# Rotating the scanned states on GpSimd in two halves per part, with four products of a half ahead of its difference and sum

## What is computed

```
u = h.astype(F32).reshape(n, l, N_SSM_GROUPS, SSM_GROUP)
bu_re = jnp.einsum('nlgc,gpc->nlgp', u, bb_re)
bu_im = jnp.einsum('nlgc,gpc->nlgp', u, bb_im)
...
_, _, xr, xi = lax.associative_scan(complex_affine_combine, (a_r, a_i, bu_re, bu_im), axis=1)
y = (jnp.einsum('nlgp,gcp->nlgc', xr, c_re.astype(F32))
     - jnp.einsum('nlgp,gcp->nlgc', xi, c_im.astype(F32)))
...
z = jax.nn.gelu(y).astype(h.dtype)
zz = z @ w_glu
```

## Time and profile before

| | |
|---|---|
| median of 3 runs | 1167.6 us (1167.45 to 1169.94) |
| the profiled execution's own time | 1169.49 us |
| its span, first to last instruction | 1167.7 us |
| busy over the span: PE | 1116.0 us (96%) |
| DVE | 725.3 us (62%) |
| ACT | 458.3 us (39%) |
| POOL | 397.2 us (34%) |
| mean granted TensorE clock | 0.990 |

### The profile page before, as it was taken

The page is one execution under the profiler, slowest core; times in us unless marked ns, Lnnn a source line. Parts: engine busy times, 40 slices in busy tenths (PEclk is TensorE's granted clock), DMA queues, the critical chain, the costliest instruction groups (busy, mean ns, idle before and its releaser), DMA issues. The chain is left out here.

```text
span 1167.7 us, 25260 instructions
## 1 busy us (share of the span) xinstructions
PE 1116.0 (96%) x9826; PEld 1092.5 (94%) x9826; DVE 725.3 (62%) x1132; ACT 458.3 (39%) x752; POOL 397.2 (34%) x624
## 2 busy tenths in 40 slices
PE   5999879999999999799998889999999999999998
PEld 5998669999999999799997779999999999999998
DVE  5874745688875258877436944457777433777632
ACT  5424773454442134344344333335444312444310
POOL 7013007999998879700337840000000000000000
PEclk9998999999999999899999999999999999999999
DMA  8322002333353332423756523222223322222322
GB/s 260 127 73 65 2 1 75 132 119 126 128 190 136 122 122 77 144 90 110 271 154 192 135 86 99 90 90 72 92 95 102 112 69 90 90 90 90 117 86 100
DMA packets 47959, 129.05 MB, mean 111 GB/s; under 512 B 12320, under 2 KB 17680, under 8 KB 47904
## 3 DMA queue, kind: packets, MB, share of 16 engines
q1 hardware_dynamic: 42272, 114.68, 30.1%
q0 software_dynamic: 5632, 13.63, 3.7%
HBM read 109.79 MB, written 18.21 MB: 110 GB/s over the span
## 5 line engine op out<-in xcount | busy, mean ns | idle before, releaser
L1547 PE MATMUL ps<-hx_hi,w_hi 128*128 128x260 f32 x1600 | 457.4, 286 | 22.5 <-DVE w_lo L1032 18.4
L1549 PE MATMUL ps<-hx_hi,w_lo 128*128 128x260 f32 x1600 | 454.4, 284 | 0.0
L1548 PE MATMUL ps<-hx_lo,w_hi 128*128 128x260 f32 x1600 | 453.2, 283 | 0.0
L722 ACT ACTIVATE w_hi<-w_raw 128x1024 fp32r<-128x1024 f32 (+1 forms) x156 | 175.6, 1126 | 445.7 <-PE ps L1549 441.4
L1547 PEld LDWEIGHTS ps<-hx_hi,w_hi 128*128 128x128 f32 x1600 | 303.7, 190 | 25.9 <-DVE w_lo L1032 11.9
L1549 PEld LDWEIGHTS ps<-hx_hi,w_lo 128*128 128x128 f32 x1600 | 303.6, 190 | 0.0
L1548 PEld LDWEIGHTS ps<-hx_lo,w_hi 128*128 128x128 f32 x1600 | 303.5, 190 | 0.1
L1032 DVE TENSOR_TENSOR w_lo<-w_raw,w_hi 128x1024 fp32r<-128x1024 f32 (+1 forms) x156 | 208.6, 1337 | 98.1 <-ACT w_hi L722 97.9
L1547 PE MATMUL ps<-hid_hi,w_hi 128*128 128x260 f32 x704 | 199.1, 283 | 0.5 <-DVE hid_lo L1372 0.5
L1548 PE MATMUL ps<-hid_lo,w_hi 128*128 128x260 f32 x704 | 198.7, 282 | 0.0
L1549 PE MATMUL ps<-hid_hi,w_lo 128*128 128x260 f32 x704 | 198.7, 282 | 0.0
(11 more groups left out here) (284 smaller groups left out, 1576.3 us busy)
## 6 DMA issues: line engine op xcount, KB each, us to landing
w_raw<-in_wup SPq DMA_DIRECT2D x88, 512.0 KB, 3.3
w_raw<-in_wdn SPq DMA_DIRECT2D x32, 704.0 KB, 4.1
w_raw<-in_wglu SPq DMA_DIRECT2D x16, 512.0 KB, 3.4
w_raw<-in_wqkv SPq DMA_DIRECT2D x12, 512.0 KB, 3.4
w_raw<-in_wo SPq DMA_DIRECT2D x8, 512.0 KB, 3.3
g_scr<-rec POOLq DMA_DIRECT2D x8, 512.0 KB, 3.1
c_scr<-rec POOLq DMA_DIRECT2D x8, 512.0 KB, 3.3
wst<-g_scr SPq DMA_DIRECT2D x8, 512.0 KB, 7.7
```

The source lines that it names most:

```text
L722: act.activation(w_hi[b][:, 0:kt * P], w_raw[b][:, 0:kt * P], ACT.Copy).then_inc(hi_done, 1)
L1547: pe.matmul(out, wh, xh, start=(k == 0), stop=False)
L1548: pe.matmul(out, wh, xl, start=False, stop=False)
L1549: ins = pe.matmul(out, wl, xh, start=False, stop=(k == kt - 1))
```

## The change

The six instructions of a part's rotation on POOL, each over 256 columns, become twelve over 128 columns. The part is cut into two halves of two pairs of groups (`h` 0 and 1). In a half all four products are issued, into four separate pieces of `ptmp`; then POOL waits for them once; then come the difference and the sum. The first half ends in a wait of POOL for its own sum, since the second half writes the same pieces of `ptmp`; the second half's sum gives `x_done`. The copy that follows, the loop over the parts and every other engine's list stay as they are. `ptmp` has 512 columns before and after.

```
-                t0 = ptmp[:, 0:JQ * 64].rearrange("p (q c) -> p q c", q=JQ)
-                t1 = ptmp[:, JQ * 64:JQ * 128].rearrange("p (q c) -> p q c", q=JQ)
-                out = x4[:, JQ * j:JQ * (j + 1), :, NS + 1:NS + 1 + NC]
                 pool.wait_ge(sem("z_done"), j + 1)
                 tt = pool.tensor_tensor
-                tt(t0, z[:, 0], e[0], ALU.mult)
-                after(tt(t1, z[:, 1], e[1], ALU.mult))
-                after(tt(out[:, :, 0, :], t0, t1, ALU.subtract))
-                tt(t0, z[:, 1], e[0], ALU.mult)
-                after(tt(t1, z[:, 0], e[1], ALU.mult))
-                tt(out[:, :, 1, :], t0, t1, ALU.add).then_inc(sem("x_done"), 1)
+                for h in range(2):
+                    g = slice(2 * h, 2 * h + 2)
+                    z = zst[j % 2][:].rearrange("p (r q c) -> p r q c", r=2, q=JQ)[:, :, g]
+                    e = [t[:].rearrange("p (q c) -> p q c", q=JQ)[:, g] for t in rots[j % ROTS]]
+                    t0, t1, t2, t3 = [ptmp[:, n * 128:n * 128 + 128].rearrange("p (q c) -> p q c", q=2)
+                                      for n in range(4)]
+                    out = x4[:, JQ * j + 2 * h:JQ * j + 2 * h + 2, :, NS + 1:NS + 1 + NC]
+                    tt(t0, z[:, 0], e[0], ALU.mult)
+                    tt(t1, z[:, 1], e[1], ALU.mult)
+                    tt(t2, z[:, 1], e[0], ALU.mult)
+                    after(tt(t3, z[:, 0], e[1], ALU.mult))
+                    tt(out[:, :, 0, :], t0, t1, ALU.subtract)
+                    ins = tt(out[:, :, 1, :], t2, t3, ALU.add)
+                    if h == 0:
+                        after(ins)
+                    else:
+                        ins.then_inc(sem("x_done"), 1)
```

More of the change, by code:

```diff
@@ L693, in _ @@
             for j in range(NJ):
-                z = zst[j % 2][:].rearrange("p (r q c) -> p r q c", r=2, q=JQ)
-                e = [t[:].rearrange("p (q c) -> p q c", q=JQ) for t in rots[j % ROTS]]
-                t0 = ptmp[:, 0:JQ * 64].rearrange("p (q c) -> p q c", q=JQ)
-                t1 = ptmp[:, JQ * 64:JQ * 128].rearrange("p (q c) -> p q c", q=JQ)
-                out = x4[:, JQ * j:JQ * (j + 1), :, NS + 1:NS + 1 + NC]
                 pool.wait_ge(sem("z_done"), j + 1)
                 tt = pool.tensor_tensor
-                tt(t0, z[:, 0], e[0], ALU.mult)
-                after(tt(t1, z[:, 1], e[1], ALU.mult))
-                after(tt(out[:, :, 0, :], t0, t1, ALU.subtract))
-                tt(t0, z[:, 1], e[0], ALU.mult)
-                after(tt(t1, z[:, 0], e[1], ALU.mult))
-                tt(out[:, :, 1, :], t0, t1, ALU.add).then_inc(sem("x_done"), 1)
+                for h in range(2):
[15 more added lines that the diff above has]
+                        ins.then_inc(sem("x_done"), 1)
                 pool.wait_ge(sem("x_done"), j + 1)
```

## The result

The changed kernel takes 1171.64 us (median of 20 runs, 1168.32 to 1172.84), the kernel before 1168.74 us (median of 20, 1167.24 to 1170.18). The ratio is 1.0023, with a 95% interval of 1.0016 to 1.0030. The change makes the kernel slower by 2.7 us; I had forecast 1173.6 us, 6.0 us above the median of the three runs then known.

A forecast was written before the change was run, and what follows sets the result against it. DVE was taken to pace the stage, POOL to become the bound. Eight parts 43.5, gaps 2.3 and disturbances 11.5 us end rotations at 691.9, starting the GLU 5.7 us later; with half the clock loss, 1173.6 us, range 1167.8 to 1178.

The forecast's parts named there:

- DVE pacing the kernel before; POOL with 2.3 us of room: State-space stage: DVE sets the pace; POOL's last rotation ends at 683.95, PE needs it at 686.31, 0.29 us a part.
- The path over part 6: End of the stage, PE and ACT: 5.5 us a part, less than POOL's 5.77 for part 7, so adding nothing.
- 0.92 us more for POOL in every part: POOL's rotation undisturbed: twelve half-width instructions take 5.44 us a part against 4.52 for six.
- Gaps of 0.33 us between parts: POOL between rotations: the copy plus 0.08 us until the next part starts, seven gaps making 2.3 us.
- Disturbances of 11.5 us: DVE holding POOL in parts 1 to 7: 14 sums 3.5, 14 scans 5.6, four `scale_u` 2.4 us.
- DVE gets most of its 6.8 us back, and waits it away: DVE regains most time lost to POOL, but from about part 4 its scan waits for a `zst` buffer.
- PE at the lower clock behind longer idle times: PE's C matmuls of the last part may run slow, adding 0.7 us; half was put in.
- The rival of the faster kernel: DVE stays the bound and recovers most of 6.8 us through shorter POOL instructions: 1162 us; chance 0.10.
- The rival of no change: POOL's later end uses up little more than its 2.3 us room, disturbances at most some 8 us: 1168.8; chance 0.14.

The follow-up runs named there:

- order-only run: Kernel before with the four products ahead of the difference and sum, still 256 columns wide, six instructions a part: ratio 0.9993.
- PSUM edit: DVE's second product placed in free PSUM columns, so its sum and difference have one SBUF input: 0.9971 on the kernel before, 1.0000 on the changed kernel, both against before.
- six small copies: Kernel before plus an 8-column copy on GpSimd ahead of each of a part's six rotation instructions, width and order unchanged: ratio 1.0019.
- quarters: Changed kernel cut further, into four rounds of 64 columns, 24 instructions a part: ratio 1.0185 to the kernel before.
- halves only: Kernel before with twelve 128-column instructions in its old order (two products, difference, two products, sum) and a wait at each step: ratio 1.0056.

## Why the prediction was right, and where its sizes were off

The mechanism came as forecast, POOL's own time per part turning the pace over, but the size did not: 6.0 us forecast against 2.7 measured. That 1173.6 lies only 2.0 us above the measured 1171.64 is in part luck: the median of 20 runs of the kernel before is 1.1 us above the median of three from which I had counted.

**DVE pacing the kernel before; POOL with 2.3 us of room.** Right. The order-only run takes 0.23 us a part off POOL and gains nothing that can be told; the PSUM edit takes time off DVE and gains 3.4 us. The rotations grew by 54.28 - 49.40 = 4.88 us, and 4.88 - 2.3 = 2.6 of it reached the GLU (2.73 measured). The path over part 6, put at 5.5 us and at adding nothing, came out level with POOL: it takes 5.6 us, and from part 6's last sum to part 7's POOL takes 5.58.

**0.92 us more for POOL in every part.** Nearly: 0.85 us. Its last part takes 5.37 us, not 5.44, since a wait is worth about 0.07 us of empty time and not 0.08, and 128 columns take 0.455. Over eight parts this is 0.6 us of the error.

**Gaps of 0.33 us between parts.** Too much: the copy's start to the next product's start is 0.15 us, because `z_done` long stands and nothing is waited for there. A gap is 0.21 us, 0.8 us less over seven. This term was mis-sized in kind: I took a restart after a wait for a case in which I had just argued that POOL no longer waits.

**Disturbances of 11.5 us.** The main term, and too large: POOL's rotations took 54.28 us, of which 8 x 5.37 + 7 x 0.21 = 44.4 are its own, so 9.9 us were taken by DVE. A scan held it for 0.42 and 0.37 us in part 6, as I had put in (0.40). The sums held it for 0.06 to 0.28, most often 0.18, where I had taken 0.25, on the ground that they could arrive while POOL is between two instructions. By the PSUM edit they cost 2.1 us in all, not 3.5. That leaves 7.8 us for scans and `scale_u`, near the 8.0 put in. The three terms together are 0.6 + 0.8 + 1.6 = 3.0 us, the whole difference between the 57.3 us that the rotations were to take and the 54.3 that they took. All three err the same way.

**DVE gets most of its 6.8 us back, and waits it away.** Half right. The sum and the difference got 3.6 us back. That the narrower instructions did this, as I had argued, is not shown: with the six small copies, where POOL's products and sums keep their 256 columns, the same two instructions take 551 and 583 ns, as short as the 537 and 617 of the changed kernel. In both runs POOL hardly waits for DVE (4.8 and 5.4 us in all, 4.7 us or more of it at the first rotation), so that the two meet at other moments than before; what shortened the waits stays open. The scans lost 1.2 us more, because POOL is now busy beside them and its next instruction comes in between the two scans of a pair. DVE's loss fell from 6.8 to 4.4 us. I had also named the wrong place for its new wait. It does not stand at the scan for want of a `zst` buffer; it stands ahead of its first product:

```profile
669.82 1.48 DVE L1504 TENSOR_TENSOR_SCAN zst<-sq,vrot 128x256 f32<-128x256 f32 x2
672.62 0.42 DVE L1487 TENSOR_TENSOR vtmp<-ps,rot 128x256 f32<-128x256 f32 x1 [1.32 <-issue]
```

and in PE's timeline of the same kernel stands what it waits for:

```profile
669.39 1.97 PE L1910 MATMUL ps<-recs,xst 64*72 64x128 f32 x32 [1.14 <-POOL xst L709]
671.29 1.22 PE L1877 MATMUL ps<-u_in,wst 128*64 128x72 f32 x32
```

DVE's part 7 needs `states_in(7)` (L1877, in flight until 672.51), which PE has in its list behind the C matmuls of part 4, and those wait for POOL's rotation of part 4. DVE's part 6 had stood 0.90 us in the same way, until 665.87, for the `states_in(6)` that PE had in flight until 665.77. I had worked out that path and set it aside as having room. It has room against POOL's pace, so the time is right all the same, but it is the first to hold DVE. Only in the quarters does DVE's scan wait for POOL's rotation (5.7 us in 4 waits).

**PE at the lower clock behind longer idle times.** It was put in with half its price, and did not come at the end. PE idled 0.80 to 1.46 us ahead of the C matmuls of six parts, and its clock stayed up there; only those of part 0, after 2.30 us, ran low (granted clock 0.50 from 642 to 644 us). With halves only the C matmuls of part 0 stayed at 1.97 us after 2.49 us of idle time, so the idle time alone does not decide it. The slow ones cost nothing here, since the chain that ended last stands on POOL at that time:

```profile
640.95 3.14 PE L1910 MATMUL ps<-recs,xst 64*72 64x128 f32 x32 [2.30 <-issue]
```

**The rival of the faster kernel.** What it needs did happen: DVE's waits at the sum and the difference fell from 382 to 157 ns on average, over the 420 ns that these take alone (with the six small copies they fell to 147, so the width need not be the reason). It does not decide, since what paces the kernel after the change is GpSimd's own list. **The rival of no change** was close. The disturbances came to 9.9 us against the 8 at which it begins, and its border of 0.2% lies inside the measured interval, 0.16 to 0.30%. That the kernel is slower is clear; that it is slower by more than 0.2% is not.

## What to carry to other kernels

Before a list of instructions on GpSimd is cut finer, multiply the added instructions by their fixed time (some 0.15 us from start to start here) and compare it with the engine's idle time per round; 0.85 us against 0.68 us of idle time and 0.29 us of room was enough to turn the pace over. Where VectorE and GpSimd hold each other, look for which VectorE instructions have both inputs in SBUF: moving one input of two of them to free PSUM columns was worth 3.4 us without touching GpSimd. To tell which of two engines paces a stage, take time off each in a run of its own, and read in the changed profile who still waits for whom.

## What the runs showed of the hardware

In this stage a DVE product, sum or difference of 256 columns with one input in PSUM was not lengthened by GpSimd in any run, even with GpSimd busy beside it: 0.41 to 0.43 us for each of them, where the same sum with both inputs in SBUF took up to 0.95 us. The Trainium skill (SBUF — State Buffer, Who interferes with whom) states that a DVE instruction with at most one SBUF input, outside the 2-port modes, does not contend with GpSimd, and that one with two contends with a GpSimd instruction that reads SBUF. These runs agree. What I had not expected is that the hold works out so differently with phase. A pair of scans beside a busy GpSimd lets one GpSimd instruction in between its two halves: from part 2 on the pair took 1.75 to 1.89 us with 256-column neighbours (the kernel before with DVE's product in PSUM) and 1.47 to 1.76 us, most often 1.48, in the changed kernel, against 1.26 alone. So one engine's gain at one place comes back as a loss at another.
